# Heads' steps spread over the quarters of a projection, and weights' lower halves on VectorE apart from their upper halves

## The reference, cut to what matters

```python
h = rms_norm(x, g_attn[layer])
proj = h @ w_in[layer]
aq, ak, av, iq, ik, iw, bq, bk, bv = jnp.split(proj, SPLIT_OFFSETS, axis=-1)
aq = partial_rope(rms_norm(aq.reshape(b, s, A_HEADS, A_HEAD_DIM), g_qa[layer]), cos, sin)
...
y_a = dsa_mixer(aq, ak, av, iq, ik, iw, k_sel).reshape(b, s, A_HEADS * A_HEAD_DIM)
...
y_b = diff_mixer(q1, q2, k1, k2, bv, lam, lam_init, g_subln[layer]).reshape(b, s, B_HEADS * B_V_DIM)
x = x + jnp.concatenate([y_a, y_b], axis=-1) @ w_o[layer]
x = x + moe(rms_norm(x, g_ffn[layer]), w_router[layer], b_router[layer],
            w_gu[layer], b_gu[layer], w_down[layer], b_down[layer])
```

## Time and profile before

| | |
|---|---|
| median of 3 runs | 1588.65 us (1587.66 to 1590.91) |
| the profiled execution | 1579.26 us, its span 1577.4 us |
| first matmul of the expert part | at 410.2 us of the span |
| busy, share of the span | PE 93%, DVE 83%, ACT 70%, POOL 18% |
| matmuls of the experts (L1826), share of the last chain | 67% |
| POOL on lower halves of weights (L525) | 16 instructions, 38.7 us |
| a piece of weights, 512 KB, from issue to landing | 3.7 us |
| VectorE, small pieces, starts to starts | sums 0.8 us, rotation 0.9, `combine` 0.95, a search round 1.0 (256 keys) or 1.2 (384) |
| ScalarE, an exponential with its sum | 0.57 us |

### The profile page before, as it was taken

How to read it: one execution, slowest core, us unless ns; L and a number is a source line. 1 busy time by engine, 2 the same in 40 slices (tenths; PEclk the granted TensorE clock), 3 DMA queues, 4 the chain that set the end, 5 groups by cost and what they waited for, 6 DMA issues and landing times.

```text
span 1577.4 us, 18729 instructions
## 1 busy us (share of the span) xinstructions
PE 1467.5 (93%) x7095; PEld 1205.3 (76%) x7098; DVE 1314.8 (83%) x1290; ACT 1102.0 (70%) x1188; POOL 280.9 (18%) x144
## 2 busy tenths in 40 slices
PE   6887876998789999999999999999999999999996
PEld 5765664776568888888888888888888888888885
DVE  5687657644879999999999999999999999998994
ACT  5554445443568778788878877788778877888773
POOL 1533201001111111211112111211112111211101
PEclk9999995998799999999999999999999999999998
DMA  6321001116899999999999999999999999999991
GB/s 193 84 65 41 27 28 53 41 41 233 289 304 365 365 363 372 368 367 375 369 370 371 375 351 368 374 370 371 366 376 369 374 352 369 370 368 358 381 363 39
DMA packets 99244, 448.66 MB, mean 284 GB/s; under 512 B 18368, under 2 KB 19520, under 8 KB 66304
## 3 DMA queue, kind: packets, MB, share of 16 engines
q1 hardware_dynamic: 87264, 428.39, 70.3%
q0 software_dynamic: 9792, 18.90, 5.0%
q10 hardware_dynamic: 2080, 0.01, 0.1%
HBM read 440.95 MB, written 23.07 MB: 294 GB/s over the span
## 4 chain that ended last, share of the span: by engine, by line
PE 84%; DVE 9%; ACT 4%; issue 2%; DMA 0%; POOL 0%; SPq 0%; ACTq 0%; POOLq 0%; DVEq 0%
PE ps L1826 67%; PE ps L1609 2%; PE ps L1611 2%; PE ps L1610 2%; PE ps L1836 2%; PE ps L1795 2%; PE ps L1616 2%; PE ps L1787 2%; PE ps L1705 1%; DVE work L1294 1%; DVE ss L1238 1%; DVE nmax L1316 1%; ACT W L930 1%; DVE work L1305 1%; DVE top L1304 1%
## 5 line engine op out<-in xcount | busy, mean ns | idle before, releaser
L712 DVE TENSOR_TENSOR whl<-wraw,whl 128x2048 fp32r<-128x2048 f32 x384 | 865.7, 2289 | 87.7 <-ACT whl L707 79.8
L707 ACT ACTIVATE whl<-wraw 128x2048 fp32r<-128x2048 f32 x384 | 732.5, 1918 | 207.7 <-PE ps L1826 207.7
L1826 PE MATMUL ps<-whl,xT 128*128 128x512 f32 x3120 | 734.1, 393 | 2.9 <-DVE xT L1517 1.6
L1826 PEld LDWEIGHTS ps<-whl,xT 128*128 128x128 f32 x3120 | 583.2, 189 | 125.1 <-issue 2.4
L1826 PE MATMUL ps<-whl,aT 128*128 128x512 f32 x1488 | 345.9, 391 | 0.0
L1826 PEld LDWEIGHTS ps<-whl,aT 128*128 128x128 f32 x1488 | 277.0, 188 | 56.2 <-DVE whl L712 0.3
L876 POOL DMA_INDIRECT out_dram<-ysb,idx x32 | 100.7, 3145 | 450.7 <-ACT ysb L1141 450.7
L867 POOL DMA_INDIRECT xg<-h_rows,idx x32 | 89.2, 2787 | 474.6 <-DVE idx L1505 454.4
L1609 PE MATMUL ps<-W,HT 128*128 128x512 f32 (+1 forms) x184 | 73.7, 400 | 1.7 <-DVE HT L1214 1.7
L1009 ACT ACTIVATE raw<-ps,nmax 128x384 f32<-128x384 f32 (+2 forms) x40 | 24.1, 602 | 69.9 <-DVE nmax L1316 69.8
L1611 PE MATMUL ps<-W,HT 128*128 128x512 f32 (+1 forms) x184 | 70.5, 383 | 0.0
(11 more groups left out here) (243 smaller groups left out, 1390.7 us busy)
## 6 DMA issues: line engine op xcount, KB each, us to landing
wraw<-in_w_gu_dram SPq DMA_DIRECT2D x256, 1024.0 KB, 8.0
wraw<-in_w_down_dram SPq DMA_DIRECT2D x128, 1024.0 KB, 7.0
WR<-in_w_in_dram SPq DMA_DIRECT2D x20, 512.0 KB, 3.7
WR<-in_w_o_dram SPq DMA_DIRECT2D x8, 512.0 KB, 3.7
xs<-in_x_dram SPq DMA_DIRECT2D x4, 512.0 KB, 6.1
WR<-in_x_dram SPq DMA_DIRECT2D x4, 512.0 KB, 3.3
out_dram<-WR SPq DMA_DIRECT2D x4, 512.0 KB, 2.6
h_rows<-WR SPq DMA_DIRECT2D x4, 512.0 KB, 2.6
```

Of the source, the lines that this page charges most:

```text
L707: act.activation(whl[:, n % HL, 0, :], wraw[n % RAW], ACT.Copy).then_inc(chunk_hi, 1)
L712: eng.tensor_tensor(whl[:, n % HL, 1, :], wraw[n % RAW], whl[:, n % HL, 0, :].bitcast(F32), ALU.subtract).then_inc(chunk_lo, 1)
L1826: ins = pe.matmul(bank, a[x_][j], w[:, b, j, 512 * q:512 * q + 512], start=c == NG and j == 0 and n == 0, stop=last and j == nj - 1 and n ...
```

## The change

`make_plan` writes the front part in another order, and pieces 8 to 23 lose their GpSimd path.

- `split_w` becomes two entries, `w_hi` (ScalarE) and `w_lo` (VectorE, all 32 pieces). In a step `w_hi` stands in quarter 0, `w_lo` in quarter 1. In units 24 to 31 `w_hi` m comes behind `combine`, and the lower half one unit later.
- `split_heads` becomes `heads_hi` (quarter 1) and `heads_lo` (quarter 2), for the item two back (three for `bk`).
- ScalarE's part of `sums` becomes `square`, ahead of the quarters and behind `turn_heads`; VectorE's stays `sums`, now in quarter 0. `norm` goes to quarter 2 and `rope` to quarter 3, both of the item one back, where they were of the item two back.

```diff
-POOL_SPLITS = range(8, 4 * WO)
...
-        if n >= 24 and pieces:
-            plan.append(pieces.pop(0))
         if product_of(n - 1) and product_of(n - 1)[0] == "B":
             plan.append(("combine", product_of(n - 1)))
+        if n >= 24:
+            if pieces:
+                plan.append(("w_hi", pieces.pop(0)))
+            if 4 * WO <= n - 25 + 4 * WO < 4 * (WO + 2):
+                plan.append(("w_lo", n - 25 + 4 * WO))
...
         fill = ATTEND_AT.get(s, 0)
+        all_of("turn_heads", back(3, not_bk) + back(4, only_bk))
+        all_of("square", back(1))
         for q in range(PARTS):
             if s < n_items:
                 plan.append(("proj", s, q))
...
+            if q == 0:
+                now = []
+                while s < n_items and pieces and pieces[0] <= 4 * ITEMS[s][0] + 4 + ITEMS[s][1] \
+                        and pieces[0] < 4 * WO:
+                    now.append(pieces.pop(0))
+                all_of("w_hi", now)
+                all_of("sums", back(1))
+            if q == 1:
+                all_of("heads_hi", back(2, not_bk) + back(3, only_bk))
+                all_of("w_lo", now)
+            if q == 2:
+                all_of("norm", back(1))
+                all_of("heads_lo", back(2, not_bk) + back(3, only_bk))
+            if q == 3:
+                all_of("rope", back(1))
             if s < n_items and q < (3 if s < 16 else 2):
                 next_search(1)
...
-                if st[0] == "split_w" and st[1] in POOL_SPLITS:
-                    if st[1] == POOL_SPLITS[0]:
-                        pool.wait_ge(w_lo, st[1])
-                    split_w_lo(pool, st[1])
```

More of the change, by code:

```diff
@@ L116, in make_plan @@
 def make_plan():
-    pieces = [("split_w", m) for m in range(4 * (WO + 2))]
+    pieces = list(range(4 * (WO + 2)))
     plan = []
     for k in range(0, KD, 2):
-        plan += [("turn_h", k), ("turn_h", k + 1), pieces.pop(0)]
+        m = pieces.pop(0)
+        plan += [("turn_h", k), ("turn_h", k + 1), ("w_hi", m), ("w_lo", m)]
     plan += [("setup",)]
@@ L156, in make_plan, with back, all_of, not_bk @@
     for s in range(n_items + 3):
-        norm = 0 <= s - 2 < n_items and has_heads(s - 2)
-        if norm:
-            plan.append(("norm", s - 2))
-        if s < n_items:
-            while pieces and pieces[0][1] <= 4 * ITEMS[s][0] + 4 + ITEMS[s][1] and pieces[0][1] < 4 * WO:
-                plan.append(pieces.pop(0))
-        if 0 <= s - 1 < n_items and has_heads(s - 1):
-            plan.append(("sums", s - 1))
-        if norm:
-            plan.append(("rope", s - 2))
-        def late_by(d):
-            u = s - d
-            if not 0 <= u < n_items or not has_heads(u):
-                return None
-            return CHUNKS[ITEMS[u][0]][0] == "bk"
-        if late_by(3) is False:
-            plan.append(("turn_heads", s - 3))
-        if late_by(4):
-            plan.append(("turn_heads", s - 4))
-        if late_by(2) is False:
-            plan.append(("split_heads", s - 2))
-        if late_by(3):
-            plan.append(("split_heads", s - 3))
+        def back(d, keep=lambda name: name != "bv"):
+            u = s - d
+            return [u] if 0 <= u < n_items and keep(CHUNKS[ITEMS[u][0]][0]) else []
+        def all_of(kind, us):
+            for u in us:
+                plan.append((kind, u))
+        def not_bk(name):
+            return name not in ("bk", "bv")
+        def only_bk(name):
+            return name == "bk"
         fill = ATTEND_AT.get(s, 0)
+        all_of("turn_heads", back(3, not_bk) + back(4, only_bk))
+        all_of("square", back(1))
         for q in range(PARTS):
@@ L821, in _ @@
             for st in PLAN:
-                if st[0] == "split_w" and st[1] in POOL_SPLITS:
-                    if st[1] == POOL_SPLITS[0]:
-                        pool.wait_ge(w_lo, st[1])
-                    split_w_lo(pool, st[1])
-                elif st[0] == "sums" and st[1] in NORMED:
+                if st[0] == "sums" and st[1] in NORMED:
                     u = st[1]
@@ L924, in _ @@
                        .then_inc(hi_ok, 1)
-                elif kind == "split_w":
+                elif kind == "w_hi":
                     m = st[1]
@@ L931, in _ @@
                        .then_inc(w_hi, 1)
-                elif kind == "sums" and st[1] in NORMED:
+                elif kind == "square" and st[1] in NORMED:
                     u = st[1]
@@ L951, in _ @@
                                    scale=xroot[:, ITEMS[u][1]:ITEMS[u][1] + 1]).then_inc(raw_ok, 1)
-                elif kind == "split_heads":
+                elif kind == "heads_hi":
                     u = st[1]
@@ L1216, in _ @@
                                              op1=ALU.subtract).then_inc(turn_read[g % 2], 1)
-                elif kind == "split_w" and st[1] not in POOL_SPLITS:
-                    if st[1] == POOL_SPLITS[-1] + 1:
-                        dve.wait_ge(w_lo, st[1])
+                elif kind == "w_lo":
                     split_w_lo(dve, st[1])
@@ L1269, in _ @@
                        .then_inc(roped, 1)
-                elif kind == "split_heads":
+                elif kind == "heads_lo":
                     u = st[1]
```

## The result

The changed kernel takes 1567.82 us (median; 1566.74 to 1569.26) where the kernel before takes 1588.16 us (1578.89 to 1590.91). The ratio is 0.9889 with a 95% interval of 0.986 to 0.9918: 20 us faster, and 3.8 us above the forecast of 1564. A second comparison (e9) gave 0.986 (0.984 to 0.9881).

The account below looks back on a forecast made before the run. VectorE paces steps 10 to 14, waits in turn bind steps 15 to 18, and a chain of waits units 24 to 31; +1.1 - 0.9 - 1.6 - 12.6 - 0.5 - 10.1 = -24.6 us from 1588.65 gives 1564 us, range 1550 to 1580.

Parts of the forecast that it names:

- `kvi`: Steps 3 to 6: a new loop through turning, copies, splits and heads' lower halves takes 20.1 us, +1.1 us.
- steps 10 to 14: The block goes but a new turning loop closes: 52.5 us where it was 54.1, -1.6 us.
- steps 15 to 18: Work spread over quarters no longer holds up row maxima: 40.1 us for 52.7, -12.6 us.
- steps 19 to 22: Costed at nothing because TensorE fills them, with half a us off for bank waits: -0.5 us.
- units 24 to 31: Lower halves a unit later end the serial chain: 28.5 us falls to 17.2; -10.1 us counting 1.23 in unit 32.
- from unit 32 on: The last lower half, 1.23 us, now falls in unit 32, where VectorE is the pace.
- GpSimd to VectorE, "level": Sixteen lower halves add 1.23 us each to VectorE, but stalls of about 1.3 us a step go: load about level.
- Only the units win: Rival: VectorE answers row maxima late in any order, steps 15 to 18 give 3 us; -13, 1576 us; chance 0.15.
- The loop doesn't bind: Rival: VectorE keeps ahead of the turning loop, so steps and units gain more; -35, 1554 us; chance 0.15.
- The root locks VectorE: Rival: each GpSimd root holds up VectorE by 1.2 us in steps it paces; -12, 1577 us; chance 0.03.
- Slower by the clock: Rival: TensorE's idle lumps at step starts halve its clock in steps 10 to 18; +18, 1607 us; chance 0.05.
- the forecast's loop: Steps 10 to 13: from heads' lower halves over turning, matmuls and score back to VectorE, 3.3 to 3.5 us.

Follow-up runs that it names:

- e9: The changed kernel run and timed once more, nothing edited: median 1565.36 us, ratio 0.986 to the kernel before.
- e5: The changed kernel with both halves of the `bk` heads moved to quarter 0, where the kernel before has them: 1562.42 us, one execution.
- e6: The changed kernel with the squares moved ahead of the turned copies on ScalarE: 1563.56 us, one execution.
- e2: The kernel before with GpSimd's sixteen lower halves moved to VectorE, old order kept: 1578.11 us, one execution.
- e3: The changed kernel with the lower halves of pieces 8 to 23 back on GpSimd: 1578.32 us, one execution.
- e4: The changed kernel, heads except `bk`: upper halves moved to quarter 0, lower halves to the start of quarter 1: 1552.03 us, one execution.
- e12: The kernel before with all lower halves on VectorE and the changed units 24 on, but the old order of steps: 1570.92 us, ratio 0.9896.
- e1: The kernel before with only units 24 on as changed, steps and GpSimd's splits as before: 1571.26 us, one execution.

## Why the prediction was right, and where it was not

The time lay in the range and on its side, and no rival happened as a whole. That it came within 4 us of 1564 is in part luck: the front part gave 16.7 or 17.5 us of the 24.6, and the medians moved by 20.3. By steps, in the changed kernel's two traces:

| term | forecast | measured |
|---|---|---|
| `kvi`, turning to turning | +1.1 | +1.7, +0.9 |
| steps 7 to 9 | -0.9 | -0.6, -0.6 |
| steps 10 to 14 | -1.6 | -0.5, -0.7 |
| steps 15 to 18 | -12.6 | -10.8, -10.8 |
| steps 19 to 22 | -0.5 | **+5.0, +4.9** |
| units 24 to 31 | -11.3 | -13.1, -13.1 |
| from unit 32 on | +1.2 | +1.9, +2.5 |
| front part | -24.6 | -16.7, -17.5 |

The lines leave some 0.3 and 0.5 us of the front part over, since they don't meet exactly: the `kvi` line goes from turning to turning and the others from eviction to eviction, and steps 0 to 2 have no line.

**The step that failed** is the sentence that costed items 19 to 22 at nothing because TensorE fills them. It makes up 5.5 of the 7.9 us by which the sum was too large. These steps held the one move that I didn't follow: `bk`'s lower halves go from the block at a step's start to quarter 2, while their turning stays at the next step's start, the very loop that I had worked out for the other heads. I excused the stretch by TensorE's full load, but a stretch is full only in the order that it was measured in: TensorE's idle time there went from 2.6 to 5.7 us. e5 gives the loss back by moving the `bk` halves alone, and e6 shows that it isn't the squares' place on ScalarE.

**GpSimd to VectorE, "level".** Too careful: e2 alone is a gain of 4.3 us in the old order, and in the new one e3 puts the engine's change at 9.7. The scaling went to 0.17 us as said. The Trainium skill, page "Perfetto Trace Analysis", section "Optimizing Scalar/DVE Operations", says that a saturated VectorE may better give work away; by that alone steps 10 to 14 would have grown by 6.1 us, and e2's shrank by 2.1. The prediction read the section too narrowly: it goes on to say that GpSimd and VectorE share a port for reading SBUF, so that moving work between these two might not help, and that part the trace bears out: 2.04 us for a VectorE instruction of 0.62 beside a split.

**`kvi`.** 20.1 us forecast, 20.7 and 60.09 - 40.14 = 19.95 measured. The difference between the two traces is one turning, 1.92 us instead of 1.09, and what follows it at the low clock. e4's 15.3 us between evictions, for 19.2 and 18.4, shows the loop behind this number.

**Steps 10 to 14.** The mechanism was right, though in steps 11 to 14 and not 10 to 13; the waits of turning were 2.4 to 2.8 us and under the 3 us that would have spoken against it. The steps took 8.7, 10.4, 10.8, 12.5 and 11.1 us for a forecast of 10.4, 10.7, 11.2, 11.2 and 9.0: in step 14 I let the loop end, since there are no more indexer scores, but the lower half that its turning needs is written in step 13's quarter 2, and TensorE waited 2.81 us once more (row at 127.35). Step 13 is over by 1.3 us, and there eight matmuls ran at the low clock, which took about 1.7 us more than at the full one (3.50 us for 8 x 0.23). Step 10 was shorter by 1.7.

**Steps 15 to 18.** 41.9 for 40.1: 10.6, 11.3, 12.4 and 7.6 us for 9.4, 10.8, 10.3 and 9.5. The sum was near, the split between steps wasn't; step 18 isn't held by VectorE. e2, e3 and e12 show the cause that I named, the block: without the spreading these steps take 52 to 55 us with the splits on either engine, and with it 42 to 44.

**Units.** The pair loop is 4.2 us and not 4.6. I had both numbers: VectorE's own work, 4.2, and a chain through TensorE and ScalarE that I estimated from low-clock durations at 4.6, and took the longer. The row at 230.23 has VectorE idle 0.35 us a pair; the chain was over-estimated. Their 13.1 us lie outside my own bounds for the units, 8 to 12. My sign for it, maxima spaced by under 2.3 us, was wrong too: within a pair they are 1.5 and 2.7 us apart.

**Rivals.** "Only the units win" put steps 15 to 18 at -3 us, they gave 10.8. "The loop doesn't bind": e4 is near to what its world looks like, and there the front part is at 379.2. "The root locks VectorE": in the changed kernel a root of 1.64 us began at 98.03, and the score that VectorE began at 98.84, well inside it, took 0.62 us, as without one. "Slower by the clock": it happened once in the forecast's loop, in step 13, after a wait of 2.58 us and so short of the 3 us that I had named, and again in step 19; the granted clock from 80 to 188 us was 0.97 even so.

**What stays open.** The medians differ by 20.3 and 21.5 us, the front parts by 16.7 and 17.5. The kernel before has one trace, from an execution 9 us below its median. e1 shares its order up to step 22, and its one trace repeats the stretches of steps 3 to 22 within 0.2 us each. Whether the slower executions of the kernel before lose their 9 us in the front or in the expert part can't be read, since none of them has a trace.

## What to carry to other kernels

A block that is spread over a step must be followed one item at a time to who waits for it first: what is due at the next step's start goes into the earliest quarter, whatever engine seems free. A stretch that is full in the trace of before is no cover for an edit that moves its own operands. When a change has parts, cost each alone and then the sum: here the part that moved most of the code was worth the least until two of its items were put a quarter earlier.
